# Hybrid mixer of a two-block transformer on one Trainium2 core: the second pair of decay blocks moved behind the seventh head's scores on TensorE and ScalarE

## The reference, cut to what matters

```python
def causal_attention(q, k, v):            # per head, blocks of 128 queries
    sc = einsum('bhqd,bhkd->bhqk', qi, k) * scale
    sc = where(kpos <= qpos, sc, min)
    p = softmax(sc)
    return einsum('bhqk,bhkd->bhqd', p, v)

def ssd_chunked(x, dt, a, bm, cm):        # 4 chunks of 128 tokens, 8 heads of 64
    acs = cumsum(dt * a)                  # within a chunk
    lmat = exp(where(tri, acs_l - acs_s, -inf))
    scores = einsum('bclhn,bcshn->bclsh', cc, bc) * lmat
    y_diag = einsum('bclsh,bcshp->bclhp', scores, xc)
    ...                                   # states carried from chunk to chunk
    y_off = einsum('bclhn,bchpn,bclh->bclhp', cc, prev, exp(acs))
    return y_diag + y_off

def hybrid_mixer(h, ...):
    ...
    y = ssd_chunked(...) + d_skip * xs
    yg = rmsnorm(y * silu(z)) * ssd_norm_w
    return concatenate([attn_out, yg], axis=-1) @ w_out
```

## Time and profile before

| what | value |
|---|---|
| median of three runs | 3166.58 us (3164.78 to 3168.45) |
| profiled execution, its own time | 3168.01 us |
| its span, first to last instruction | 3166.2 us |
| PE busy | 3152.1 us (100%), 14696 matmuls |
| DVE, ACT, POOL busy | 1862.0, 1169.3, 155.5 us |
| mean granted TensorE clock | 0.999 |
| first mixer's changed part | about 2135 to 2165 us of the span |
| second mixer's changed part | about 2717 to 2747 us of the span |

### The profile page before, as it was taken

One profiled execution on the slowest core, in us unless ns is written; L12 is line 12 of the kernel. 1 busy time (PEld: TensorE's weight loads), 2 busy tenths in 40 slices (PEclk: granted clock), 3 DMA queues, 4 the chain that ended last, 5 costly groups with the idle time before them and its releaser, 6 DMA issues.

```text
span 3166.2 us, 36001 instructions
## 1 busy us (share of the span) xinstructions
PE 3152.1 (100%) x14696; PEld 2600.2 (82%) x14696; DVE 1862.0 (59%) x2673; ACT 1169.3 (37%) x1643; POOL 155.5 (5%) x170
## 2 busy tenths in 40 slices
PE   9999999999999999999999999999999999999999
PEld 7888878888888888888888888877888888788887
DVE  6774367666447664357666635987433358763332
ACT  4332254322233222263322223566322235742221
POOL 2000000000000000000000000131000002300000
PEclk9999999999999999999999999999999999999999
DMA  6443322444333443322244432221222332022322
GB/s 175 147 146 123 99 85 90 134 148 151 117 110 107 150 150 117 102 93 81 93 147 134 151 115 96 84 67 53 92 95 90 100 89 80 28 93 93 107 87 74
DMA packets 334331, 339.79 MB, mean 107 GB/s; under 512 B 12502, under 2 KB 329208, under 8 KB 334168
## 3 DMA queue, kind: packets, MB, share of 16 engines
q1 hardware_dynamic: 332144, 333.80, 32.9%
q0 software_dynamic: 1792, 3.62, 0.5%
q10 hardware_dynamic: 232, 0.06, 0.0%
HBM read 335.36 MB, written 2.10 MB: 107 GB/s over the span
## 4 chain that ended last, share of the span: by engine, by line
PE 92%; DVE 5%; ACT 3%; issue 0%; DMA 0%; POOL 0%; SPq 0%; DVEq 0%; POOLq 0%
PE ps L138 90%; ACT ar L95 1%; PE ps L141 1%; DVE ar L108 1%; DVE wl L100 1%; DVE ar L100 1%; ACT wh L95 0%; DVE sp L100 0%; ACT sp L95 0%; DVE small L120 0%; ACT L95 0%; DMA ar<-in_x 0%; DVE ada L108 0%; DVE ar L111 0%; ACT T L95 0%
## 5 line engine op out<-in xcount | busy, mean ns | idle before, releaser
L138 PE MATMUL ps<-hh,wl 128*128 128x512 f32 x2760 | 1082.4, 392 | 1.6 <-DVE wl L100 1.2
L100 DVE TENSOR_TENSOR wl<-raw,wh 128x1024 fp32r<-128x1024 f32 (+3 forms) x549 | 655.0, 1194 | 726.1 <-ACT wh L95 725.2
L138 PE MATMUL ps<-hh,wh 128*128 128x512 f32 x2760 | 1075.2, 390 | 0.0
L138 PE MATMUL ps<-hl,wh 128*128 128x512 f32 x2760 | 1074.6, 389 | 0.0
L95 ACT ACTIVATE wh<-raw 128x1024 fp32r<-128x1024 f32 (+3 forms) x549 | 561.8, 1025 | 506.0 <-PE ps L138 504.8
L138 PEld LDWEIGHTS ps<-hh,wl 128*128 128x128 f32 x2760 | 518.5, 188 | 113.5 <-issue 6.9
L138 PEld LDWEIGHTS ps<-hh,wh 128*128 128x128 f32 x2760 | 518.4, 188 | 108.9
L138 PEld LDWEIGHTS ps<-hl,wh 128*128 128x128 f32 x2760 | 518.7, 188 | 105.3 <-issue 0.4
L138 PE MATMUL ps<-ul,wh 128*128 128x512 f32 x1152 | 440.5, 389 | 0.0
L138 PE MATMUL ps<-uh,wl 128*128 128x512 f32 x1056 | 411.6, 390 | 0.0
L138 PE MATMUL ps<-uh,wh 128*128 128x512 f32 x1056 | 411.0, 389 | 0.0
(11 more groups left out here) (251 smaller groups left out, 2677.0 us busy)
## 6 DMA issues: line engine op xcount, KB each, us to landing
raw<-in_ffn_w SPq DMA_DIRECT2D x119, 1024.0 KB, 5.3
raw<-in_w_ada SPq DMA_DIRECT2D x48, 1024.0 KB, 5.2
raw<-in_w_gate_up SPq DMA_DIRECT2D x44, 1024.0 KB, 5.1
raw<-in_m_w_in SPq DMA_DIRECT2D x26, 1024.0 KB, 5.3
raw<-in_w_down SPq DMA_DIRECT2D x16, 1024.0 KB, 4.9
raw<-in_ffn_w SPq DMA_DIRECT2D x16, 768.0 KB, 4.2
raw<-in_w_in SPq DMA_DIRECT2D x12, 1024.0 KB, 5.4
raw<-in_m_w_out SPq DMA_DIRECT2D x8, 1024.0 KB, 5.0
```

Of the source, the lines that this page charges most:

```text
L100: return self.issue(lambda e: e.tensor_tensor(out, a, b, op))
L138: return self.issue(lambda e: e.matmul(out, l, r, start=start, stop=stop, skip_group_check=True))
```

## The change

On PE and ACT the call of `between()` that runs `weigh(1)` moves from the end of head 5's round (behind `turn(4)`) to head 6's round, right behind `scores(6)`. DVE had that order before. Both layers' mixers run this code. No instruction is added, taken away or changed in size; the banks change with the order of the takes: `scores(6)` now takes 4, 5, 6 and `weigh(1)` 7, 0, 1, and all others keep theirs.

```diff
@@ -1257,6 +1257,8 @@   (pe_program, mix2)
                 for hd in range(8):
                     scores(hd)
+                    if hd == 6:
+                        between()
                     if hd < 7:
                         heads_turned(hd + 1)
                     if hd in (3, 5, 7):
@@ -1264,7 +1266,8 @@
                     between()
                     if hd:
                         turn(hd - 1)
-                    between()
+                    if hd != 5:
+                        between()
                 between()
                 turn(7)
@@ -2014,7 +2019,7 @@
                     between()
                     if hd:
                         turn(hd - 1)
-                    if hd < 7:
+                    if hd not in (5, 7):
                         between()
```

## The result

| | before | changed |
|---|---|---|
| median | 3166.41 us (6 runs) | 3175.69 us (3172.03 to 3180.38, 6 runs) |
| ratio | | 1.003, 95% interval 1.002 to 1.004 |
| profiled execution, own time | 3168.01 | 3177.38 |
| its span | 3166.2 | 3175.6 |
| mean granted TensorE clock | 0.999 | 0.996 |

The change costs 9.3 us, 0.3%. That is the forecast sign and more than double the forecast size (3.9 us); 3175.69 lies 1.7 us above the top of the range. One run of before in this comparison took 5951.94 us; it is left out of the ratio. The kernel changed was run five more times later (median 3177.68, ratio 1.0033, 1.0021 to 1.0046), so the size is no accident of the first six.

What follows compares the result with a forecast made beforehand. In the changed part of each mixer the bound was the chain through DVE and ACT, with PE waiting for them; 2 x 1.93 = 3.9 us of delay took the median from 3166.58 to 3170.5 us, range 3166.0 to 3174.0.

Steps and rivals of the forecast that it cites:

- PE wins 2.0 us for `scores(6)`, of which 0.6 reach DVE: In each mixer `scores(6)` starts 2.0 us sooner on PE; DVE's minima of head 6 start only 0.6 us sooner.
- ACT's `weigh(1)` starts 2.02 us later; DVE's products end 1.93 us later; DVE stands still for 2.4 us: Per mixer, ACT does head 6's exponentials (2.02 us) before `weigh(1)`'s; DVE waits about 2.4 us, its products end 1.93 later.
- PE waits 1.4 to 1.5 us for ACT before `scores(7)`: PE waits 1.4 to 1.5 us for banks that ACT's late `turn(5)` copies leave, reaching `turn(6)` at 2159.4, not 2157.96.
- The clock: TensorE's granted clock around the new pause before `scores(7)`: the sum charged nothing; one fall per mixer would make 3.9 us 7.3.
- by the row of the pause the clock holds: PE busy 1.97 of 2.50 us around the old wait before `scores(6)` kept clock 1.00, so the sum stays 3.9 us.
- PE meets them at the `frames(2)` product, 2162.2 now: PE rejoins late ACT and DVE at the `frames(2)` product, 2160.26 before; all three are then 1.93 us late.
- Rival C: The clock falls in one or both mixers, adding 1.7 or 3.4 us: 3172.2 to 3173.9 us; chance 0.10.
- The rule cited beside the clock: TensorE rotating PSUM banks with short stops can be thrown between clock levels; by it the cost would be 7.3 us.
- A: PE's bank wait was the bound: PE wins 0.5 to 0.9 us per mixer, 3165.2 us, not slower; chance 0.10.
- B: DVE's delay is swallowed by the minima's 0.6 us and ACT's waits; PE ends as before, 3166.6 us; chance 0.10.
- D: The shifted order saves a clock fall such as that at 2218 us, 1.7 us: 3168.8 us; chance 0.06.

Runs made afterwards that it cites:

- filled: The changed kernel with twenty extra matmuls in all, rewriting the same values in TensorE's waits in `weigh(1)` and `weigh(2)`; median 3172.63 us.
- act_only: Only ACT takes the new order, PE keeps the order of the kernel before; median 3173.0 us, 6.6 over before.
- dve_moved: The changed kernel, but DVE does `frames(0)` first and its products of `weigh(1)` behind it; median 3170.92 us.
- shifted: The kernel before with nine repeated 512-column matmuls in the first block's last feed-forward, moving the second block later, no wait changed; median 3169.90 us.
- pe_only: Only PE takes the new order, ACT keeps the order of the kernel before; median 3173.83 us, ratio 1.0022.
- paused: The kernel before with one more PE wait ahead of `scores(7)`, for ACT's square of `frames(1)`; median 3172.6 us, 6.2 over before.
- first_only: The new order in the first mixer only, the second as in the kernel before; median 3170.1 us, 3.7 over before.
- second_only: The new order in the second mixer only, the first as in the kernel before; median 3170.4 us, 3.6 over before.

## Why the prediction was right or wrong

- **PE wins 2.0 us for `scores(6)`, of which 0.6 reach DVE.** Right: the 0.62 us before the minima is gone and the minima follow the products without a wait.
- **ACT's `weigh(1)` starts 2.02 us later; DVE's products end 1.93 us later; DVE stands still for 2.4 us.** Right: 2.01, 2.04 and 2.51 us. filled shows 2.04 us per mixer in the total, so nothing gave it back and nothing else was added.
- **PE waits 1.4 to 1.5 us for ACT before `scores(7)`.** Right: 1.59, and ACT as releaser; `scores(7)` starts 1.73 us later against `turn(4)`. A second wait that I had not reckoned stands before `frames(1)`, 0.59 us, for ACT's `weigh(1)` (bank 0). It costs nothing by itself, as DVE and ACT set the end, but it adds to TensorE's idle time ahead of the falls.
- **The clock. This is the step that failed.** The sum took it at nothing, "by the row of the pause the clock holds", and gave a fall in one or both mixers a chance of 0.10. What the sum rested on, that row, had one pause of under a microsecond; the changed kernel has one of about 0.9 and one of 1.8 between matmul starts, within 7 us. Measured, in two profiles of the changed kernel: 1.0, 2.7, 2.7 and 2.7 us per mixer beyond the stall, with one portion of low clock in the first and two in the others. The step "PE meets them at the `frames(2)` product, 2162.2 now" failed with it: the slow matmuls made TensorE the last one there, 3.02 us late in the first mixer in place of 1.93, while ACT was 2.05 late.
- **What a fall costs there.** One portion of 1.7 us costs 1.0 in the first mixer, since TensorE had 0.8 us of room: `scores(7)` alone was late by 1.73 where DVE and ACT were by 2.04, and from `turn(6)` (3.47 late) to the product (3.02) another 0.45 came off. Rival C was the right mechanism: its 3.4 us for both mixers, 1.7 in each, stand against 3.6 measured in the first profile and 5.4 in the second. That it comes near the first is luck, for one mixer took 1.0 and the other 2.7. Its 3173.9 is still short of the medians, 3175.7 and 3177.7, and both profiles have falls outside the mixers too.
- **The rule cited beside the clock.** By the Trainium skill, "TensorE: Matmul & The Clock Gate", section "A second HAM failure mode: psum-queue depth-cycling", a TensorE that often stands still for moments between its groups of matmuls goes back and forth between the two levels (seen there in a bf16 kernel). The changed kernel's windows agree (0.66 and 0.50 behind the pauses, 1.00 again later). act_only and dve_moved, whose TensorE stands still between bank groups as well (1.49 and 0.49 us; 0.59 and 0.57 us), kept 1.00 in their mixers. What makes the difference is open.
- **The rest.** Of 9.4 us in span, 4.1 is the stall, 3.6 the clock in the mixers, and 1.7 a fall at 172 us that stands ahead of the change. Over medians it is less sharp: the kernel's runs spread over 8.4 us with mean clocks from 0.998 down to 0.995, and the fastest, 3172.03 at 0.998, is 1.5 us above the sum of the forecast. filled, with no fall in the mixers of its profile, still has a median 2.1 us above before plus stall, and shifted 1.4 above before plus its matmuls; so a part of the median's excess lies outside the mixers. How much is not settled.
- **A and B** fell: nothing swallowed the stall, and the bank wait was not the bound (it is gone, and the kernel is slower). **D** is half seen: the fall at 2218 is missing in the first profile of the changed kernel, present in the second.

## What to carry to other kernels

When an order is changed on one engine and the other two are brought into line, look at what overlapped before: here VectorE took a head's minima while ScalarE took the blocks' exponentials, and "the same order everywhere" turned that overlap into a wait. Follow every swapped PSUM bank to its next taker, not only the group that moved. And price a new pause of TensorE twice, once for its length and once for the clock: that one shorter pause left the clock at full speed is no reason to price the fall at nothing. Here all six mixers profiled with the full new order had a fall, at 1.0 to 2.7 us each; of the six profiled with other pauses of 1.5 us or more (pe_only, act_only, paused), one had, though nine of eleven runs of paused had a lower mean clock. So give such a fall a term of its own and a large share of the chance, where I gave it a tenth.

## What the runs showed of the hardware

- The low clock came in portions that cost 1.7 us of full-speed work each. The times of the kernel before gather about as far apart (near 3165.0, 3166.6 and 3168.4), at mean clocks of 1.0 for the lowest and 0.999 for the others, with some runs between the first two.
- One portion appeared at 172 to 180 us in five of the twelve profiles (changed, pe_only, first_only, second_only, shifted), in a part of the program that is the same in all of them. The two profiles of the changed kernel differ in it, so two executions can do so with no change at all.
- Repeating matmuls nobody needs, twenty of them in TensorE's waits, made a kernel 3.1 us faster; the clock in its mixers stayed at 1.00.
- The same pauses did not always bring a fall: behind a wait of 2.34 us the clock stayed at 1.00 in one mixer of pe_only and fell to 0.57 (2732 to 2736) in the other, in one execution.
- After a fall within the mixer a second portion could follow at once (0.50 in 2740 to 2744, 0.65 in 2744 to 2748), while TensorE did its small matmuls; filled, with no such pause, had none in either mixer.
